# Queries and keys of the neighbourhood layer by seven products, one product per step of two row tiles

## The reference

```
proj = a @ w_in                                # a: 1024 tokens x 1024
q, k, v, mq = split(proj, [768, 1536, 2304])   # 12 heads of 64
s = q . k (window of 8 rows x 16 columns) + relative bias, masked
p = softmax(s);  o = p . v
```

## Time and profile before

| | us |
|---|---|
| median of 3 runs (2205.24 to 2205.95) | 2205.66 |
| the profiled execution's own time | 2205.68 |
| its span, first to last instruction | 2203.9 |
| PE busy | 2187.2 (99%) |
| DVE busy | 1295.4 (59%) |
| POOL busy | 1179.5 (54%) |
| ACT busy | 924.2 (42%) |

### The profile page before, as it was taken

The page is one execution under the profiler, slowest core; times in us unless marked ns, Lnnn a source line. Parts: engine busy times, 40 slices in busy tenths (PEclk is TensorE's granted clock), DMA queues, the critical chain, the costliest instruction groups (busy, mean ns, idle before and its releaser), DMA issues.

```text
span 2203.9 us, 31940 instructions
## 1 busy us (share of the span) xinstructions
PE 2187.2 (99%) x11542; PEld 1797.4 (82%) x11542; DVE 1295.4 (59%) x2161; ACT 924.2 (42%) x1851; POOL 1179.5 (54%) x951
## 2 busy tenths in 40 slices
PE   9999999999999999999999999999999999999998
PEld 8778888888888888888889877778878888888887
DVE  7896666657544444676853255554675434447767
ACT  6633233365233232344663355464723233234454
POOL 1276655678988888200334433416798878870001
PEclk9999999999999999999999999999999999999999
DMA  8011112553343333743453533335433433348334
GB/s 334 30 39 48 63 53 87 172 189 97 135 161 102 101 108 98 285 158 97 130 161 106 151 74 74 82 125 186 148 105 122 147 115 101 100 129 316 97 99 163
DMA packets 130970, 280.37 MB, mean 127 GB/s; under 512 B 31983, under 2 KB 46590, under 8 KB 128766
## 3 DMA queue, kind: packets, MB, share of 16 engines
q1 hardware_dynamic: 130814, 278.33, 38.8%
HBM read 207.76 MB, written 70.54 MB: 126 GB/s over the span
## 4 chain that ended last, share of the span: by engine, by line
PE 93%; POOL 3%; ACT 1%; DVE 1%; issue 1%; DMA 0%; SPq 0%; DVEq 0%; POOLq 0%; ACTq 0%
PE PS L2724 28%; PE PS L2726 28%; PE PS L2725 27%; PE PS L2999 2%; POOL OPS L1116 2%; PE PS L3265 2%; PE PS L3247 1%; PE PS L3165 1%; PE PS L2986 1%; PE PS L3032 1%; POOL TW L1140 1%; PE PS L3152 1%; PE PS L3176 0%; PE PS L3178 0%; PE PS L3180 0%
## 5 line engine op out<-in xcount | busy, mean ns | idle before, releaser
L2724 PE MATMUL PS<-AOP,OPS 128*128 128x512 f32 x1216 | 474.4, 390 | 1.1 <-POOL OPS L1116 0.6
L2726 PE MATMUL PS<-AOP,OPS 128*128 128x512 f32 x1216 | 473.2, 389 | 0.0
L2725 PE MATMUL PS<-AOP,OPS 128*128 128x512 f32 x1216 | 473.2, 389 | 0.0
L1116 POOL TENSOR_TENSOR OPS<-TW,OPS 128x512 fp32r<-128x512 f32 x174 | 263.0, 1526 | 78.6 <-ACT OPS L1487 77.3
L1050 POOL TENSOR_TENSOR wlo<-stage,whi 128x512 fp32r<-128x512 f32 (+1 forms) x120 | 153.8, 1304 | 236.4 <-ACT whi L1380 236.2
L2724 PEld LDWEIGHTS PS<-AOP,OPS 128*128 128x128 f32 x1216 | 228.2, 188 | 51.4 <-POOL OPS L1116 2.4
L2726 PEld LDWEIGHTS PS<-AOP,OPS 128*128 128x128 f32 x1216 | 228.2, 188 | 47.4
L2725 PEld LDWEIGHTS PS<-AOP,OPS 128*128 128x128 f32 x1216 | 228.3, 188 | 47.1
L1487 ACT ACTIVATE OPS<-TW 128x512 fp32r<-128x512 f32 x176 | 106.6, 628 | 344.0 <-POOL TW L1140 321.7
L2724 PE MATMUL PS<-OPS 128*128 128x512 f32 x584 | 227.7, 390 | 0.3
L2726 PE MATMUL PS<-OPS 128*128 128x512 f32 x584 | 227.2, 389 | 0.0
(11 more groups left out here) (334 smaller groups left out, 4695.4 us busy)
## 6 DMA issues: line engine op xcount, KB each, us to landing
stage<-in_w SPq DMA_DIRECT2D x100, 512.0 KB, 3.8
hidden_scratch<-HT SPq DMA_DIRECT2D x154, 256.0 KB, 2.2
SRAW<-hidden_scratch SPq DMA_DIRECT2D x154, 256.0 KB, 2.7
stage<-in_wpack SPq DMA_DIRECT2D x76, 512.0 KB, 3.8
BW<-in_w SPq DMA_DIRECT2D x16, 1024.0 KB, 8.2
h_scratch<-Hb SPq DMA_DIRECT2D x24, 512.0 KB, 3.8
Hb<-h_scratch SPq DMA_DIRECT2D x24, 512.0 KB, 6.0
cat_scratch<-OC SPq DMA_DIRECT2D x14, 512.0 KB, 2.9
```

What stands on the lines that cost most here:

```text
L1116: pool.tensor_tensor(place[:, 1, :], w1_operand(l, j, p), place[:, 0, :].bitcast(F32), ALU.subtract)\
L2724: pe.matmul(dst, stat[0], mov[0], start=start, stop=False, skip_group_check=onto)
L2725: pe.matmul(dst, stat[0], mov[1], start=False, stop=False, skip_group_check=onto)
L2726: return pe.matmul(dst, stat[1], mov[0], start=False, stop=stop, skip_group_check=onto)
```

## The change

Pairs 2 to 5 (the fillers from T = 15 to T = 78) are no longer projected by 16 pieces of six matmuls each. Each pair's two weight units and the tokens are seen as 2 by 2 blocks (the input in two halves of 512, the tokens in two halves of 512, queries and keys), and seven products of half-size blocks (`NA_ORDER`, `pair_product`, 4 blocks of three matmuls = 12 matmuls each) replace eight. Product q stands whole in `filler(T+1)` of the q-th step of two tiles of a pair's sixteen; `filler(T)` of these steps is empty, and the eighth step (T % 16 = 14) has no filler at all. The operands are sums: POOL makes nine token sums of four tiles each before and during the first pair (`token_step`), with the high parts on ACT (`token_hi`) and low parts on DVE (`token_lo`). Per pair POOL makes four weight sums (`pair_sum`) and seven low parts (`pair_lo`), ACT seven high parts (`pair_hi`), and the results are put together by one ACT copy (`pair_one`), five DVE additions (`pair_add`) and the query copies (`pair_queries`). The bias tables of a pair are made in two halves between the low parts. SP loads the weights one unit at a time around the other loads, and fetches the first six tiles of the mixed heads after the last pair's weights. The low part of the first output operand is one tile later (`LO_AT`).

```diff
@@ -65,6 +65,12 @@
 RET_ORDER = "1627543"
 RET_PLACE = {"1": 0, "2": 0, "6": 1, "7": 2, "4": 2, "5": 3, "3": 3}
 N_RET = 14 * (RH - 1)
+NA_BLOCKS = range(U_NAH + 4, U_OUT1)
+NA_ORDER = "1726543"
+NA_BANK = {"1": 0, "2": 0, "6": 1, "7": 2, "4": 2, "5": 3, "3": 3}
+NA_SUMS = "7564"
+NA_ADDS = ("u2", "u3", "22", "21", "12")
+N_NA = 7 * (HP - 2)
 
 
...
@@ -1008,18 +1092,18 @@
             store_values(3)
             load_values(1)
             store_cat(9)
+            load_units(U_NAH + 7)
             for hp in range(1, HP):
-                if hp == HP - 1:
-                    for k in range(3):
-                        cat_back(1, 0, [k], (k_last, 2 * k + 2))
-                load_units(U_NAH + 2 * hp + 7)
                 if hp + 1 < HP:
                     load_bias(hp + 1)
+                if hp >= 2:
+                    load_units(U_NAH + 2 * hp + 5)
                 if hp == HP - 1:
-                    cat_back(1, 0, range(3, KD - 2))
+                    cat_back(1, 0, range(KD - 2), na_multiplied(HP - 3, "2"))
                 store_cat(9 + hp)
                 if hp + 1 < HP:
                     load_values(hp + 1)
+                    load_units(U_NAH + 2 * hp + 6)
             load_units(U_OUT1 + 5)
             cat_back(1, 0, [KD - 2])
             cat_back(1, 1, range(KD - 1))
...
             mask_bias(0, (2, 3))
+
+            def token_step(n, dst, a, b, op):
+
+                for k in range(4):
+                    if n:
+                        pool.wait_ge(t_sum, TS0 + 4 * n - 3 + k)
...
+
+            def pair_sum(i, p):
+
+                first, second = na_units(i)
+                b1, b2 = stage[:, w_slot(first), :], stage[:, w_slot(second), :]
+                lo, hi = slice(0, HALF), slice(HALF, 2 * HALF)
+                if p == "7":
+                    pool.wait_ge(w_in[w_slot(second)], w_come(second))
+                    a, b = b2[:, lo], b2[:, hi]
+                elif p == "5":
+                    pool.wait_ge(w_in[w_slot(first)], w_come(first))
+                    a, b = b2[:, lo], b1[:, lo]
+                elif p == "6":
+                    pool.wait_ge(*na_summed(i, "5"))
+                    a, b = b2[:, hi], na_sum_place("5")[:, :]
+                else:
+                    pool.wait_ge(*na_summed(i, "6"))
+                    pool.wait_ge(n_lo, LO0 + 7 * i + NA_ORDER.index("7") + 1)
+                    a, b = b1[:, hi], na_sum_place("6")[:, :]
+                if i == 0 and p != "4":
+                    pool.wait_ge(*USED[U_NAH + (2 if p == "7" else 3)])
+                elif p != "4":
+                    pool.wait_ge(n_lo, LO0 + 7 * i - 7 + NA_ORDER.index({"7": "4"}.get(p, p)) + 1)
+                pool.tensor_tensor(na_sum_place(p)[:, :], a, b, ALU.subtract).then_inc(n_sum, 1)
+
+            def pair_lo(q):
+
+                place = na_op[q % 3]
+                pool.wait_ge(n_hi, HI0 + q + 1)
+                pool.tensor_tensor(place[:, 1, :], na_weight(q), place[:, 0, :].bitcast(F32), ALU.subtract).then_inc(n_lo, 1)
+
+            los(U_V + 12)
+            pool.wait_ge(pre_sq, 26)
+            pool.wait_ge(a_lo, a_before(7))
+            token_step(0, one, part(1, 0, 0), part(1, 1, 0), ALU.add)
+            token_step(1, diff, one, part(0, 0, 0), ALU.subtract)
+            token_step(2, diff, diff, part(0, 1, 0), ALU.subtract)
+            los(U_NAH + 3)
+            token_step(3, one, one, part(1, 0, 4), ALU.add)
+            token_step(4, one, one, part(1, 1, 4), ALU.add)
             los(U_NAH + 4)
-            for hp in range(HP):
-                if hp + 1 < HP:
-                    mask_bias(hp + 1)
-                los(min(U_NAH + 2 * hp + 6, U_OUT1 + 2))
+            pool.wait_ge(pv, R_ROW)
+            token_step(5, two, diff, part(1, 0, 4), ALU.add)
+            token_step(6, two, two, part(1, 1, 4), ALU.add)
+            mask_bias(1)
+            pool.wait_ge(*USED[U_NAH + 2])
+            token_step(7, four, part(0, 0, 4), two, ALU.subtract)
+            token_step(8, four, four, part(0, 1, 4), ALU.add)
+            for i in range(HP - 2):
+                pair_sum(i, "7")
+                pair_lo(7 * i)
+                pair_lo(7 * i + 1)
+                for p in "564":
+                    pair_sum(i, p)
+                pair_lo(7 * i + 2)
+                if i + 2 < HP:
+                    mask_bias(i + 2, (0, 1))
+                pair_lo(7 * i + 3)
+                pair_lo(7 * i + 4)
+                if i + 2 < HP:
+                    mask_bias(i + 2, (2, 3))
+                pair_lo(7 * i + 5)
+                pair_lo(7 * i + 6)
+            los(U_OUT1 + 2)
             out_phase(1)
             ffn(1)
...
+            def pair_hi(q):
+
+                i, p = q // 7, NA_ORDER[q % 7]
+                if q < 3:
+                    act.wait_ge(*USED[U_NAH + (1, 3, 1)[q]])
+                else:
+                    act.wait_ge(n_used, USED0 + q - 2)
+                if p in "123":
+                    n = na_units(i)[1 if p == "3" else 0]
+                    act.wait_ge(w_in[w_slot(n)], w_come(n))
+                else:
+                    act.wait_ge(*na_summed(i, p))
+                act.activation(na_op[q % 3][:, 0, :], na_weight(q), ACT.Copy).then_inc(n_hi, 1)
...
+            HI_AT = {11: 0, 14: 1, 15: 2, 2: 3, 4: 4, 6: 5, 9: 6}
+
             for T in range(HP * ROWS + 4):
                 t = T - (HP - 1) * ROWS
-                if t == -2:
-                    act.wait_ge(*USED[next_unit(T)])
-                    for th in range(2):
-                        ins = act.activation(kTn[:, (HP - 1) % 2, HALF * th:HALF * th + HALF], PS[:, 2 + th, :], ACT.Copy)
-                    ins.then_inc(ev_act, 1)
                 if T < HP * ROWS:
                     probs(R_ROW + T, False)
                 if 0 <= T - 2 < HP * ROWS:
                     take_pt(R_ROW + T - 2)
-                if t < 0 and T % ROWS in (KD - 2, KD - 1):
-                    take_q(next_unit(T), qpair[:, (T // ROWS + 1) % 2, :, :], (T % ROWS - KD + 2,))
-                if t < 0 and T % ROWS in (KD - 1, ROWS - 2):
-                    his(next_unit(T) + RING + 1)
+                if T in (KD - 2, KD - 1):
+                    take_q(next_unit(T), qpair[:, 1, :, :], (T - KD + 2,))
+                if 1 <= T < 5:
+                    token_hi("7", T - 1)
+                if 7 <= T < 11:
+                    token_hi("6", T - 7)
+                if 15 <= T < 19:
+                    token_hi("5", T - 15)
+                if 19 <= T < 23:
+                    token_hi("3", T - 19)
+                i = (T + 5) // ROWS - 1
+                if 0 <= i < HP - 2 and T % ROWS in HI_AT:
+                    pair_hi(7 * i + HI_AT[T % ROWS])
+                i = T // ROWS - 1
+                if 0 <= i < HP - 2:
+                    if T % ROWS == 1:
+                        pair_one(i)
+                    if T % ROWS == 5:
+                        pair_queries(i, 0)
+                    if T % ROWS == 13:
+                        pair_queries(i, 1)
+                if t in (-5, 0):
+                    his(U_OUT1 + (1 if t else 3))
...
@@ -2692,6 +2934,30 @@
                         take_values(item[0], item[2])
                     if item == (U_NAH + 1, KD - 1):
                         take_k(U_NAH + 1)
+            def token_lo(p, k):
+
+                hi, lo = na_tokens(p, 0, k), na_tokens(p, 1, k)
+                dve.wait_ge(*token_done(t_hi, p, k))
+                if p in "76":
+                    dve.wait_ge(t_sum, TS0 + (28 if p == "7" else 32))
+                dve.tensor_tensor(lo, raw_sum(p, k), hi.bitcast(F32), ALU.subtract).then_inc(t_lo, 1)
+
+            def pair_add(i, what):
+
+                p = {"u2": "6", "u3": "7", "22": "5", "21": "4", "12": "3"}[what]
+                first, second, bank = na_keys(i, 0), na_keys(i, 1), na_bank(p)
+                dst, with_ = {"u2": (first, first), "u3": (second, first), "22": (second, second),
+                              "21": (bank, first), "12": (first, first)}[what]
+                dve.wait_ge(*na_multiplied(i, p))
+                if what == "u2":
+                    dve.wait_ge(n_one, ONE0 + i + 1)
+                else:
+                    dve.wait_ge(*na_added(i, {"u3": "u2", "22": "u3", "21": "u2", "12": "u2"}[what]))
+                dve.tensor_tensor(dst, bank, with_, ALU.add).then_inc(n_add, 1)
+
+            LO_STEPS = {"7": (8, 9, 10, 11), "6": (14, 15, 16, 17), "5": (18, 19, 20, 21), "3": (22, 23, 25, 27)}
+            ADDS_AT = {8: ("u2", "u3"), 10: ("22",), 12: ("21",), 14: ("12",)}
+
             for T in range(HP * ROWS + 4):
                 q, t = T - 4, T - (HP - 1) * ROWS
                 if q >= 0 and q % 4 == 3:
@@ -2710,8 +2976,15 @@
                     peak(R_ROW + T, T % ROWS, T // ROWS)
                 if 0 <= T - 1 < HP * ROWS:
                     normalise(R_ROW + T - 1, False)
-                if t < -2 and T % ROWS == ROWS - 2:
+                if T == ROWS - 2:
```

(124 more changed lines are left out.)

51 lines of the change are left out of this document (40 added, 11 removed).

## The result

The changed kernel takes 2211.23 us, median of 8 runs (2209.72 to 2214.13), against 2206.0 for the kernel before, median of 8 (2205.24 to 2206.78): ratio 1.0028, 95% interval 1.0019 to 1.0036. It is slower by 0.3%, where I forecast 2202.1 and called the range closed at 2210.

What follows compares the result with a forecast made beforehand. PE was taken as the bound, busy 99% of the span. A gain of 16.3 us, less 4.5 at the start and 8.2 at pair ends, gave -3.6 and 2202.1 us, range 2196 to 2210.

Steps and rivals of the forecast that it cites:

- 4.4 to 4.5: First pair's query unit: PE waits 4.4 to 4.5 us for POOL's low part behind twelve token sums; 4.5 taken.
- 2.6 lost: At T = 16: old key copy and a 0.69 us token low part delay peak(15) to 4.1, costing PE 2.6 us.
- My section on the rule: GpSimd and DVE port locking, kernel-wide: trace agreed for DVE, did not show POOL losing; the sum included no such cost.
- A full step becomes 4.29 to 4.38: Steps of two tiles with twelve matmuls: 4.29 to 4.38 us instead of 4.48, saving 0.10 to 0.19 each.
- Pair ends: T = 32, 48, 64: empty step saves 3.02 to 3.11 us, waiting for peak(15) and late values costs 1.4 each.
- The 0.25 for late values: At pair ends, values(13) wait for PT(13), copied after exp(15); 0.25 us of each 1.4 us loss.
- T = 78: 1.12 against 1.4: At T = 78 the output operand is ready at 3.0, wanted by PE's filler at 1.6: 1.4 us lost.
- less-stall rival: Pair-end chain shorter than placed: 3.5 us lost instead of 8.2, total 2197.4 us; chance 0.20.
- lower end 2195.8: Whole kernel, lowest sum of bounds: 17.8 us gained with 4.4 + 3.5 lost.
- Covers: Full steps and product operands: costs set at nothing; values fit by a tenth, low parts 1.9 us or more ahead.
- values without cover: Rival: PT(T-3)'s copy comes later than PE's values in 28 full steps; 0.3 late each gives 2210.5 us; chance 0.13.
- POOL slow: Rival: POOL sums at 1.53 us from contention, start wait 7.5, ACT's sum late, total 2206.4 us; chance 0.16.

Runs made afterwards that it cites:

- b_wait12: The kernel before plus twelve POOL additions into a spare tile ahead of the first pair's query unit's low part; 2211.61 us, ratio 1.0026.
- b_wait10: The kernel before plus ten such POOL additions instead of twelve, at the same place; 2207.49 us, ratio 1.0007.
- e2: The changed kernel plus 18 overwritten matmuls before PE's wait for the first query unit's low part; 2210.57 us, ratio 1.0022 to the kernel before.
- g3: f1 plus six overwritten matmuls before PE waits for tile 15's peak at T = 16; 2203.72 us, ratio 0.9989 to the kernel before.
- e1: The changed kernel with the first pair's low parts placed between POOL's token sums, each ahead of its need; 2205.91 us, ratio 1.0002 to the kernel before.
- f2: e1 with products in halves of six matmuls, one after each turn, tiles 14 and 15 of a pair empty; 2203.65 us, ratio 0.9991 to the kernel before.
- g1: f1 with the output operand's first low part ahead of the last key addition on DVE at T = 78; 2203.62 us, ratio 0.9988 to the kernel before.
- f1: e1 with one of DVE's token-sum low parts moved from index 14 to 13; 2203.52 us, ratio 0.9991 to the kernel before.

## Why the prediction was wrong, point by point

**"4.4 to 4.5" at the start: the wait was right, its price wasn't.** It is 4.07 long, released by POOL's low part, with token sums at 1.26 and 1.27, as the row of 1.28 said. The failed step is "so it stands 4.4 to 4.5 us, and everything behind moves by as much". Behind moves by 6.6 in the profile: 4.07 of wait and 2.4 of matmuls at the lower clock. b_wait12 against b_wait10 shows the surplus without the change, e2 and g3 show that it goes when PE is kept busy. In the medians the start is worth 5.3 (e1), 5.7 by the ratios.

**"2.6 lost" at T = 16 was short in two terms.** The chain was right, but its low part was put at 0.69 and took 1.72: +1.0 in the wait. The row that the 0.69 came from (`up<-PS,u`) has PS as one of its inputs and never took more than 0.69; the low part reads two tiles in SBUF. Then came 1.67 to 2.7 us of low clock in the next step, the same missing term as at the start; g3 takes it away. My section on the rule had the reason for the 1.72. The Trainium skill (SBUF — State Buffer, "SBUF: two separate sides") lets the one of GpSimd and DVE that holds the pair block the other; I left both directions out of the sum. The instances of this case, two rows each from the views of two source lines (min/median/max ns):

```profile
L2943 DVE TENSOR_TENSOR na_lo<-na_raw,na_hi x4: 1280/1760/1775, 1291.2 to 1299.7; 128x512 fp32r<-128x512 f32 x4
L2943 DVE TENSOR_TENSOR na_lo<-na_raw,aT x4: 678/682/687, 1319.3 to 1324.9; 128x512 fp32r<-128x512 f32 x4
L1454 POOL TENSOR_TENSOR na_raw<-aT x4: 1267/1278/1347, 1221.5 to 1225.2; 128x512 f32<-128x512 f32 x4
L1454 POOL TENSOR_TENSOR raw_four<-aT,raw_two x4: 1328/1535/1737, 1291.9 to 1296.6; 128x512 f32<-128x512 f32 x4
```

The same instruction of DVE takes 0.68 or 1.76, the same of POOL 1.28 or 1.54, and the long ones stand where both run such work (1291 to 1300). The trace now agrees on both sides.

**"A full step becomes 4.29 to 4.38": wrong, and the largest term.** 27 of the 28 full steps gain nothing (+0.6 together, predicted -3.9). The unseen passage, turn to scores, was bounded from above by 0.22; it is 0.31, as long as the matmul to scores that it replaces (0.32 start to start). My upper bound was put together from two other passages, and no row held it. In the first full step of a pair another 0.24 goes between values and turn (4.72 against 4.48). The values there start 0.49 after the scores, as before; it is the turn that waits, for DVE's normalising of 1.35 beside POOL's low part (T = 32 above; 48 and 64 have the same). In f2 a normalising as long (1.38) ends 0.9 before the turn, since there six matmuls of a product stand in front of the scores, and the step takes 4.48.

**Pair ends: right, by the chain that was placed.** Predicted 3 x (-3.07 + 1.4) = -5.0, measured -5.40. From the scores of tile 14, peak(15) ends at 2.81 (2.8 placed) and the next scores start at 2.97 (2.9 placed); PE's idle time in front of them is shared by the turn of tile 13 (0.56) and the scores (0.16). The 0.25 for late values did not come; the late turn of the next step, above, took its place. T = 78: 1.12 against 1.4, with a wait of 1.0, for which the view names no releaser; it falls to 0.67 in g1, where DVE makes the operand's low part first. The less-stall rival's bottom, "about 0.5 a place, 3.5 in all", was added up wrongly: five places give 2.5, so its 2197.4 and the lower end 2195.8 were each 1.0 too high.

**Covers: nearly right.** No product waits for its operand in the changed kernel, and the values of full steps don't wait: the rivals "values without cover" and "less stall" are out. "POOL slow" is half right: its last eight token sums took 1.5, but its sum for ACT is in time, so what was paid is DVE's delay. T = 0 to 14 lost 0.67, 0.54 of it at T = 12, where a turn stands 0.46 for the normalised tile behind a DVE low part of 1.76 beside POOL's sums. T = 80 to 94 lost 0.51 with the 0.60 for DVE's peak at T = 84, behind a low part of the output operand that took 1.78, where before it took 0.68. So says the trace; no run took these two apart.

**The sum.** -3.6 against +7.5: the start 2.1, T = 0 to 14 0.7, T = 14 to 16 1.2, the clock after it 2.8, full steps 4.5, others -0.2. Two reasons carry it: a wait cost more than its length, twice, and a saving in a passage that no row showed was counted 28 times. The range failed with them, since its upper end had neither a price behind a wait nor a full step without gain.

## What to carry to other kernels

A wait that empties PE for some microseconds costs its length and then a stretch at the lower clock: here 4.1 us of waiting cost 5.7 to 6.6, and 1.6 us in the midst of dense matmuls only itself; behind a step of small matmuls 1.5 us was not free. In an engine's queue the operand that PE needs next goes ahead of early work. A saving that is repeated 28 times needs a row of its own passage; without one its lower bound is zero. And where DVE and POOL both work on two SBUF inputs at the same time, both should be priced at their long duration, here 1.76 and 1.54, and DVE's normalising beside POOL at 1.35, not 0.35.

## What the runs showed that I had not expected

- After 4.06 to 4.07 us of idle PE seven matmuls (b_wait12) and twelve (the change) ran 0.43 apart (granted clock 0.50); after 1.57 us none did. But in f1 1.47 us was enough, after a step with small matmuls and turns alone, while f2, with six large matmuls between the two waits (0.56 and 1.30), kept 1.00.
- A run of scores after a turn starts 0.31 later, a 128x512 matmul after the same turn 0.13 to 0.19.
- One DVE subtraction of 128x512 tiles takes 0.68 alone and 1.76 beside POOL's additions.
